# Recurrent block in two halves: projections and gates by turns, crossing gate tiles in pairs of 64 rows, low parts and products from GpSimd to VectorE

## The chip, the cores and the metric

The kernel runs on one core of a Trainium2 chip. The metric is device time in microseconds (us) of one execution; the kernel before took 1205.96 us (median of 3 runs, 1204.94 to 1206.43). Engines are named as in the profile: PE is TensorE (PEld its weight loads), DVE is VectorE, ACT is ScalarE, POOL is GpSimd, SP issues the DMAs.

## The reference, cut to what matters

The program is one inference step of a two-layer trunk: 256 prompt tokens and 32 sample tokens, 288 columns in all, share the weights. Each layer does a half-step FFN, a mixer, a second half-step FFN and a gated per-layer embedding, with an RMSNorm ahead of each. The mixer of layer 0 is attention, that of layer 1 the recurrent block that the change rewrites:

```python
def lru_mixer(xn, h0, conv0, w_in, conv_w, conv_b, w_a, b_a, w_x, b_x, lam, w_o):
    gx = xn @ w_in                                   # D_MODEL 1024 -> 2 * D_RNN (1280 each)
    gate = jax.nn.gelu(gx[..., :D_RNN])              # "g"
    u = gx[..., D_RNN:]                              # "u"
    ext = jnp.concatenate([conv0, u], axis=1)
    c = conv_b + sum(ext[:, j:j + T] * conv_w[j] for j in range(CONV_W))      # 4 taps
    cb = c.reshape(B, T, LRU_BLOCKS, LRU_BLOCK)      # 16 blocks of 80
    r = sigmoid(einsum('btnj,njk->btnk', cb, w_a) + b_a)                      # gate a
    gin = sigmoid(einsum('btnj,njk->btnk', cb, w_x) + b_x)                    # gate x
    log_a = (-LRU_C * softplus(-lam)) * r
    a = exp(log_a)
    bterm = sqrt(-expm1(2.0 * log_a)) * (gin * c)
    bterm = bterm.at[:, 0].add(a[:, 0] * h0)
    _, h = lax.associative_scan(_lin_combine, (a, bterm), axis=1)
    y = (h * gate) @ w_o
    return y, h[:, -1], new_conv
```

## The kernel before

**Tiling.** Features lie on the 128 partitions, tokens in the free dimension. D_MODEL is 8 chunks of 128 rows, D_RNN is 10, which the gates and the scan take in two halves of 5. Convolution and gates have 292 columns, since the sample's history lies between the two groups of tokens. Every float32 product is three matmuls (`product`, L1148): high part of the weights by high part of the data (L1154), high by low (L1155), low by high (L1156). The low part of a datum is the value less its rounded copy.

**Groups of weights.** The work of all stages is a row of groups, each with 10 to 16 weight tiles of 128x128 and a slot of its own of two (`raw0`/`raw1`, `w_hi0`/`w_hi1`, `w_lo0`/`w_lo1`). For each group SP loads `raw`, ACT copies it to `w_hi` (L513), DVE subtracts to `w_lo` (L784); both do it in two parts, one group ahead of PE and interleaved by hand with the stage's own instructions. ACT may write a slot when PE is through with the group that held it (`tiles_done`), and PE starts a group's first part when the first `w_lo` stands. The order of the work on each engine is written out by hand, in one `step` function for each engine; semaphores tie the engines together.

**The recurrent block** is stage 5. Its four phases run one after the other:
- `lru_in`, 5 groups: u for two chunks each (48 matmuls). DVE scales the two products into `u_ext` (L1044, L1046), ACT starts the convolution (L663), and DVE adds three taps (L908), those of one group in the period of the next. ACT rounds the finished chunk to `c_hi` (L757), POOL subtracts to `c_lo` (L462).
- `gates`, 4 groups (a and x of the first half, a and x of the second): each is 13 tiles, 39 matmuls of 128 rows. The blocks are 80 wide, so 8 of the 13 tiles lie across a border of chunks ("crossing") and have weights in one half of their rows alone; the other 5 are a chunk's own. ACT takes the sigmoids (L685) and loads its table (L655) ahead of them.
- `lru_g`, 5 groups: g, two chunks each. Beside it run tanh, exp and sqrt of the rates on ACT (L731 to L746), squares, addend and scans on DVE (L928, L937, L921), GELU on ACT (L751), the product y on POOL (L476, L477), its high part on ACT (L761) and its low part on DVE (L914).
- `lru_o`, 8 groups of 30 matmuls: the output. Groups 0 to 3 hold two output chunks and one half of k each, so that four chunks are done after group 3; groups 4 to 7 hold one whole chunk each. Behind a finished chunk DVE adds to `x_res` (L807), ACT and DVE make the next norm's input (L518, L793), and POOL adds the squares (L388, L385).

The next phase is the FFN `up3`. Its first group takes the first 7 chunks of x for both its outputs before the last one; behind it stands the matmul of the mean of squares (L1169).

Of the kernel before, what the change touches and what calls it, by code (L numbers as in the profile page):

```python
# [11 lines left out]
P = 128  # L12
# [6 lines left out]
SEQ = 256  # L19
# [32 lines left out]
U_GROUPS = [(("u", m), ("u", m + 1)) for m in range(0, KR, 2)]  # L52
G_GROUPS = [(("g", m), ("g", m + 1)) for m in range(0, KR, 2)]
U_OF = [[m for side, m in group] for group in U_GROUPS]
GELU_AT = [range(0, 6), range(6, 8), range(8, KR)]
# [24 lines left out]
def plan():  # L80
# [4 lines left out]
    def ple(n, stage):  # L85
# [6 lines left out]
    phases += [Phase("lru_in", 5, len(U_GROUPS), 2 * KD, body=len(U_GROUPS), counted=True),  # L92
               Phase("gates", 5, 4, BAND_TILES, body=4),
               Phase("lru_g", 5, len(G_GROUPS), 2 * KD, body=len(G_GROUPS), counted=True),
               Phase("lru_o", 5, KD, KR, body=KD)]
# [10 lines left out]
QKV, WO, LRU_G = (next(p for p in PHASES if p.name == name) for name in ("qkv", "wo", "lru_g"))  # L106
# [36 lines left out]
def in_array(tile):  # L143

    for name, groups in (("lru_in", IN_FIRST), ("lru_g", IN_LAST)):
        for n, group in enumerate(groups):
            if tile in group:
                return name, n, group.index(tile)

# [17 lines left out]
def build(nc, a):  # L167
    ctx = ExitStack()
    with ctx:
# [117 lines left out]
        gate_summed, gate_read = sem("gate_summed"), sem("gate_read")  # L287
        s_done, gated_used, tanh_done, a_done = sem("s_done"), sem("gated_used"), sem("tanh_done"), sem("a_done")
        a_square_done, b_square_done, b_root_done = sem("a_square_done"), sem("b_square_done"), sem("b_root_done")
        addend_done, start_set, gap_zeroed = sem("addend_done"), sem("start_set"), sem("gap_zeroed")  # L290
# [6 lines left out]
        def group_dram(phase, i):  # L297
# [4 lines left out]
            if kind == "ple":  # L302
                return a[kind][one(i + int(layer_ffn) * phase.groups)]
            return a[phase.name][one(i)]

# [18 lines left out]
        def _(sp):  # L324
# [8 lines left out]
            for phase in PHASES:  # L333
                def load(turn, n, b, phase=phase):
# [11 lines left out]
                    if phase.kind in ("lru_in", "lru_g"):  # L346
                        for o, landed in enumerate((lru_landed, raw_landed)):
                            name, g, at = in_array((U_GROUPS if phase.kind == "lru_in" else G_GROUPS)[n][o])
                            sp.dma_start(raw[slot_of(phase, b)][:, o * KD * P:(o + 1) * KD * P],
                                         a[name][g, :, at * KD * P:(at + 1) * KD * P]) \  # L350
                                .then_inc(landed[slot_of(phase, b)], 16)
                        return
                    if phase.name in SEAMS and turn is None and n == 0:
# [26 lines left out]
        def _(pool):  # L380
# [79 lines left out]
            with pool.Fori(0, KR) as m:  # L460
                pool.wait_ge(c_hi_done, m + 1)
# [4 lines left out]
            for half in range(2):  # L466
                pool.wait_ge(a_done, half + 1)
                nc.gpsimd.memset(rate[:, half * HALF:(half + 1) * HALF, SAMPLE - 1:SAMPLE], 0.0) \
                    .then_inc(gap_zeroed, 1)

            for m in range(KR):
                pool.wait_ge(gelu_done, next(n + 1 for n, ms in enumerate(GELU_AT) if m in ms))
                pool.wait_ge(h_done, m + 1)
                if m >= HALF:
                    pool.wait_ge(y_done, m - HALF + 1)
                nc.gpsimd.tensor_tensor(y_now[m % HALF][:, 0:SEQ], u_ext[:, m, 0:SEQ], gate_g[:, m, 0:SEQ], ALU.mult)  # L476
                nc.gpsimd.tensor_tensor(y_now[m % HALF][:, SEQ:TOK], u_ext[:, m, SAMPLE:SAMPLE + DEC],  # L477
                                        gate_g[:, m, SEQ:TOK], ALU.mult).then_inc(y_prod, 1)


# [11 lines left out]
        def _(act):  # L492
            def w_split(target, part):
# [9 lines left out]
                of_lru = phase.kind in ("lru_in", "lru_g")  # L503
                if of_lru and part == 0:
                    act.wait_ge(lru_landed[slot], ((n if phase.kind == "lru_in" else len(U_GROUPS) + n) // 2 + 1) * 16)
# [72 lines left out]
            for at_phase, phase in enumerate(PHASES):  # L578
# [3 lines left out]
                def step(turn, n, b, phase=phase, after=after, stage=stage, kind=kind):  # L582
# [70 lines left out]
                    elif kind == "lru_in":  # L653
                        if n == phase.groups - 1:
                            nc.scalar.preload_act_table_set("sigmoid_and_others")  # L655
                        part(nxt, 0)
                        part(nxt, 1)
                        if n == 0:
# [3 lines left out]
                        for m in U_OF[n]:  # L662
# [3 lines left out]
                        conv_high(n - 1)  # L666
                    elif kind == "gates":
                        half, is_x = n // 2, n % 2
                        ms = slice(half * HALF, (half + 1) * HALF)
                        if n == 3:  # L670
                            act.wait_ge(gated_used, 1)
                        for m in range(HALF):
                            q = n * HALF + m
                            if m < HALF - 1:
                                act.wait_ge(gate_summed, n * (HALF - 1) + m + 1)
                            else:
                                part(nxt, 0)
                                part(nxt, 1)
                                if n == 0:
# [870 lines left out]
```

## Time and profile before

| | us |
|---|---|
| median of 3 runs | 1205.96 |
| profiled execution | 1206.72 |
| its span, first to last instruction | 1204.6 |
| PE busy | 1178.3 (98%) |
| DVE / ACT / POOL busy | 795.4 / 584.4 / 170.3 |
| from the mean in the block's first u group to the mean behind `lru_o` | 833.05 to 954.28 |

The mean granted TensorE clock is 0.993 of full speed. Of the chain that ended last 90% is PE, 5% DVE and 3% ACT, so whatever isn't a matmul counts only where PE stands still. Matmul durations are latencies: the matmuls overlap, and what one costs is the distance from one start to the next.

### The profile page before, as it was taken

What the parts mean: (1) busy time and instruction counts of PE and PEld (TensorE: products, weight loads), DVE (VectorE), ACT (ScalarE), POOL (GpSimd) and SP (SyncE); (2) the same over time, 40 slices, a digit from 0 to 9 for tenths busy, and PEclk for the clock granted to TensorE, in tenths of its full rate; (3) what the DMA queues carried; (4) which work ended last, traced back from release to release, by engine and by line L of the source; (5) the groups of instructions that cost most, each with busy time, mean ns of one, the idle gap of its engine ahead of it and who ended that gap; (6) DMA issues with size and microseconds to landing.
All of it is one profiled execution on the core that took longest, in us unless ns stands there. A gap on an engine that the chain in (4) does not pass through costs nothing.

```text
span 1204.6 us, 23286 instructions
## 1 busy us (share of the span) xinstructions
PE 1178.3 (98%) x8952; PEld 1168.4 (97%) x8952; DVE 795.4 (66%) x1170; ACT 584.4 (49%) x862; POOL 170.3 (14%) x201
## 2 busy tenths in 40 slices
PE   6999999999999999999999999999999999999996
PEld 6999999999989999999999999999999999999995
DVE  7666555677758665565785566456989856655566
ACT  6444433466645444343564444335695544443353
POOL 3000002211123000011230000021306300000222
PEclk9999999999999999999999999999999999999998
DMA  6544444743335445444455444446453554544542
GB/s 211 198 147 168 153 147 166 257 138 121 106 114 200 154 170 174 140 146 165 157 196 175 153 161 152 150 163 187 134 189 113 195 180 156 174 153 143 170 152 87
DMA packets 37627, 193.19 MB, mean 160 GB/s; under 512 B 4001, under 2 KB 6321, under 8 KB 26049
## 3 DMA queue, kind: packets, MB, share of 16 engines
q1 hardware_dynamic: 36528, 187.86, 46.5%
q0 software_dynamic: 1040, 4.51, 1.1%
q8 instruction: 42, 0.69, 0.2%
q14 instruction: 17, 0.13, 0.0%
HBM read 188.78 MB, written 3.58 MB: 160 GB/s over the span
## 4 chain that ended last, share of the span: by engine, by line
PE 90%; DVE 5%; ACT 3%; issue 1%; DMA 1%; SPq 0%; DVEq 0%; ACTq 0%
PE bank L1154 30%; PE bank L1156 29%; PE bank L1155 29%; DVE w_lo L784 2%; ACT w_hi L513 1%; DVE conv L908 1%; DMA raw<-in_up 1%; PE bank L1185 0%; DVE u_ext L921 0%; PE bank L1169 0%; DVE stay L849 0%; DVE logit L841 0%; DVE conv L937 0%; ACT stay L555 0%; ACT stay L552 0%
## 5 line engine op out<-in xcount | busy, mean ns | idle before, releaser
L513 ACT ACTIVATE w_hi<-raw 128x1024 fp32r<-128x1024 f32 (+2 forms) x410 | 370.4, 927 | 341.0 <-PE bank L1156 327.0
L784 DVE TENSOR_TENSOR w_lo<-raw,w_hi 128x1024 fp32r<-128x1024 f32 (+2 forms) x410 | 457.5, 1134 | 85.5 <-ACT w_hi L513 82.6
L1154 PE MATMUL bank<-xg_hi,w_hi 128*128 128x288 f32 x1536 | 458.8, 299 | 9.3 <-DVE w_lo L815 8.3
L1155 PE MATMUL bank<-xg_lo,w_hi 128*128 128x288 f32 x1536 | 454.5, 296 | 0.0
L1156 PE MATMUL bank<-xg_hi,w_lo 128*128 128x288 f32 x1536 | 453.0, 295 | 0.0
L1154 PEld LDWEIGHTS bank<-xg_hi,w_hi 128*128 128x128 f32 x1536 | 289.0, 188 | 11.2 <-issue 8.0
L1156 PEld LDWEIGHTS bank<-xg_hi,w_lo 128*128 128x128 f32 x1536 | 290.5, 189 | 0.0
L1155 PEld LDWEIGHTS bank<-xg_lo,w_hi 128*128 128x128 f32 x1536 | 289.7, 189 | 0.4
L1154 PE MATMUL bank<-h_hi,w_hi 128*128 128x288 f32 x704 | 208.4, 296 | 0.0
L1155 PE MATMUL bank<-h_lo,w_hi 128*128 128x288 f32 x704 | 207.7, 295 | 0.0
L1156 PE MATMUL bank<-h_hi,w_lo 128*128 128x288 f32 x704 | 207.0, 294 | 0.0
L963 DVE TENSOR_TENSOR gate_in<-bank,rstd 128x288 f32<-128x288 f32 x88 | 40.2, 457 | 177.8 <-PE bank L1156 177.6
L1156 PEld LDWEIGHTS bank<-h_hi,w_lo 128*128 128x128 f32 x704 | 132.6, 188 | 0.0
L1155 PEld LDWEIGHTS bank<-h_lo,w_hi 128*128 128x128 f32 x704 | 132.2, 188 | 0.0
L1154 PEld LDWEIGHTS bank<-h_hi,w_hi 128*128 128x128 f32 x704 | 131.9, 187 | 0.0
L1154 PE MATMUL bank<-xg_side_hi,w_hi 128*128 128x288 f32 x352 | 104.6, 297 | 0.0
L1155 PE MATMUL bank<-xg_side_lo,w_hi 128*128 128x288 f32 x352 | 103.8, 295 | 0.0
L1156 PE MATMUL bank<-xg_side_hi,w_lo 128*128 128x288 f32 x352 | 103.5, 294 | 0.0
L395 POOL TENSOR_TENSOR sum_squares<-x_res 128x288 f32<-128x288 f32 x8 | 6.2, 778 | 610.1 <-DVE x_res L807 610.1
L518 ACT ACTIVATE xg_hi<-x_res,vecs_sb 128x288 fp32r<-128x288 f32 (+1 forms) x56 | 28.9, 533 | 129.0 <-DVE x_res L807 126.0
L388 POOL TENSOR_TENSOR square<-x_res 128x288 f32 (+1 forms) x58 | 44.7, 770 | 241.6 <-DVE x_res L807 240.1
L1156 PEld LDWEIGHTS bank<-xg_side_hi,w_lo 128*128 128x128 f32 x352 | 66.3, 188 | 0.0
(185 smaller groups left out, 1246.2 us busy)
## 6 DMA issues: line engine op xcount, KB each, us to landing
raw<-in_up SPq DMA_DIRECT2D x85, 1024.0 KB, 4.9
raw<-in_down SPq DMA_DIRECT2D x64, 704.0 KB, 4.0
raw<-in_qkv SPq DMA_DIRECT2D x24, 512.0 KB, 4.6
raw<-in_ple SPq DMA_DIRECT2D x16, 640.0 KB, 3.9
raw<-in_lru_in SPq DMA_DIRECT2D x12, 512.0 KB, 4.8
raw<-in_lru_o SPq DMA_DIRECT2D x8, 640.0 KB, 3.9
raw<-in_wo SPq DMA_DIRECT2D x4, 1024.0 KB, 5.3
raw<-in_lru_g SPq DMA_DIRECT2D x8, 512.0 KB, 4.4
```

The lines of the kernel that those rows point to most:

```text
L388: nc.gpsimd.tensor_tensor(square[:], x[:, k, :], x[:, k, :], ALU.mult).then_inc(squared, 1)
L395: nc.gpsimd.tensor_tensor(sum_squares[:], x[:, 0, :], x[:, 0, :], ALU.mult).then_inc(summed_squares, 1)
L513: nc.scalar.activation(w_hi[slot][:, cols], raw[slot][:, cols], ACT.Copy).then_inc(w_hi_done, 1)
L518: nc.scalar.activation(xg_of(stage)[0][:, k, :], x[:, k, :], ACT.Copy, scale=gain[:, stage, one(k)]) \
L784: nc.vector.tensor_tensor(w_lo[slot][:, cols], raw[slot][:, cols], w_hi[slot][:, cols].bitcast(F32), ALU.subtract).then_inc(w_lo_done, 1)
L908: nc.vector.scalar_tensor_tensor(out=conv[:, m, :], in0=u_ext[:, m, tap:tap + CW], scalar=vec["conv_w"][:, one(tap * KR + m)], in1=conv[:, ...
L963: nc.vector.tensor_tensor(gate_in[:], first, rstd[:], ALU.mult).then_inc(gate_in_done, 1)
L1154: nc.tensor.matmul(out, w_hi[slot][:, cols], hi[:, k, 0:width], start=start, stop=False)
L1155: nc.tensor.matmul(out, w_hi[slot][:, cols], lo[:, k, 0:width], start=False, stop=False)
L1156: return nc.tensor.matmul(out, w_lo[slot][:, cols], hi[:, k, 0:width], start=False, stop=stop)
```

## The change

1. **Order.** The phases become `lru_in` (u0, u1, u2, g0), `gates0` (a, x of the first half), `lru_mid` (u3, u4, g1), `gates1`, `lru_g` (g2, g3, g4), `lru_o`. A half's gates, rates and scan can start before the other half's u is there. All taps of a u group are now in that group's own period.
2. **Crossing tiles in pairs.** A gate group is now 5 own tiles (15 matmuls of 128 rows) and 8 crossing tiles as 24 matmuls of 64 rows, in 12 pairs on the lower and the upper rows of the array. Rows and pairs alternate as own 0 to 3, beside 0 and 1, own 4, beside 2 and 3.
3. **POOL to DVE.** `c_low` and `y_full` (the subtraction and the product that POOL did) are DVE instructions; POOL's memset of the rates' gap goes. A scan is now two (256 and 32 columns) with `h0` as start of the second, so the copy of `h0` goes.
4. **`lru_o` by halves.** Groups 0 to 3 hold two output chunks each with the first half of k, groups 4 to 7 the same chunks with the second half. All of x's chunks are then done in groups 4 to 7, two behind each.
5. **Smaller ones.** One multiplication by a broadcast operand for five rates; GELU in two parts, not three; ACT loads 7 tables in stage 5, not 4; the weights of the block's projections land in two pieces; the first group of `up3` takes 6 chunks first, then the last 2.

```diff
-U_GROUPS = [(("u", m), ("u", m + 1)) for m in range(0, KR, 2)]
-G_GROUPS = [(("g", m), ("g", m + 1)) for m in range(0, KR, 2)]
+LRU_GROUPS = {"lru_in": (("u", 0), ("u", 1), ("u", 2), ("g", 0)), "lru_mid": (("u", 3), ("u", 4), ("g", 1)),
+              "lru_g": (("g", 2), ("g", 3), ("g", 4))}
+GATE_BANKS = (4, 5, 6, 7, 0, 1, 4, 5, 2, 3, 4, 5, 6, 7, 2, 3, 0, 1, 4, 5)
+GATE_ORDER, LAST_STEP = (0, 2, 4, 1, 3), (0, 3, 2, 3, 2)
...
+                def own(m):
+                    gate_bank_free(group, m)
+                    if tile_of[m, m] >= phase.part_a:
+                        pe.wait_ge(w_lo_done, 2 * (phase.first_group + n) + 2)
+                    pe.wait_ge(c_done, first + m + 1)
+                    product(out[m], slot, tile_of[m, m], (c_hi, c_lo), first + m, CW, True, False)
+                def beside(step, below, above):
+                    if step > 1:
+                        pe.wait_ge(beside_done, 3 * group + step - 1)
+                    for w, c in ((w_hi, c_hi), (w_hi, c_lo), (w_lo, c_hi)):
+                        for rows, (m, k) in zip(HALF_ROWS, (below, above)):
+                            cols = slice(tile_of[m, k] * P, (tile_of[m, k] + 1) * P)
+                            last = nc.tensor.matmul(out[m], w[slot][rows, cols], c[rows, first + k, :], start=False,
+                                                    stop=w is w_lo and step == LAST_STEP[m])
+                    return last.then_inc(tiles_done if step == 3 else beside_done, 1)
+                pe.wait_ge(w_lo_done, 2 * (phase.first_group + n) + 1)
+                for m in range(HALF - 1):
+                    own(m)
+                beside(0, (0, 1), (2, 1))
+                beside(1, (1, 2), (3, 2))
+                own(HALF - 1)
+                beside(2, (2, 3), (4, 3))
+                beside(3, (3, 4), (1, 0))
...
-                nc.gpsimd.tensor_tensor(c_lo[:, m, :], conv[:, m, :], c_hi[:, m, :].bitcast(F32), ALU.subtract) \
-                    .then_inc(c_done, 1)
+            def c_low(group):
+                for m in U_OF[group]:
+                    dve.wait_ge(c_hi_done, m + 1)
+                    nc.vector.tensor_tensor(c_lo[:, m, :], conv[:, m, :], c_hi[:, m, :].bitcast(F32), ALU.subtract) \
+                        .then_inc(c_done, 1)
...
 def o_chunks(n):
-    return () if n < 2 else (2 * n - 4, 2 * n - 3) if n < KD // 2 else (n,)
+    return () if n < KD // 2 else (2 * n - KD, 2 * n - KD + 1)
```

On PE, the start of a gate group before: each output bank takes its two or three tiles one after the other, all of 128 rows (lines 1154 to 1156 are `product`).

```order
L1154 MATMUL bank4<-c_hi,w_hi1 128x292
L1155 MATMUL bank4<-c_lo,w_hi1 128x292
L1156 MATMUL bank4<-c_hi,w_lo1 128x292
L1154 MATMUL bank4<-c_hi,w_hi1 128x292
L1155 MATMUL bank4<-c_lo,w_hi1 128x292
L1156 MATMUL bank4<-c_hi,w_lo1 128x292
L1154 MATMUL bank5<-c_hi,w_hi1 128x292
```

On PE, the first gate group now, from the last of its first four own tiles (lines 1231 to 1233 are `product`, 1340 is the 64-row matmul of `beside`).

```order
L1233 MATMUL bank7<-c_hi,w_lo0 128x292
L1340 MATMUL bank4<-c_hi,w_hi0 128x292
L1340 MATMUL bank6<-c_hi,w_hi0 128x292
L1340 MATMUL bank4<-c_lo,w_hi0 128x292
L1340 MATMUL bank6<-c_lo,w_hi0 128x292
L1340 MATMUL bank4<-c_hi,w_lo0 128x292
L1340 MATMUL bank6<-c_hi,w_lo0 128x292
L1340 MATMUL bank5<-c_hi,w_hi0 128x292
L1340 MATMUL bank7<-c_hi,w_hi0 128x292
```

The two matmuls of a pair write different banks, and both lie between 128-row matmuls of the same group.

On ACT, from the last u group ahead of the first gates but one to the first sigmoids, before: `c_hi` is the rounding, L655 the table, `w_hi` of 896 and 768 the weights of a gate group.

```order
L757 ACTIVATE c_hi<-conv 128x292 x2
L513 ACTIVATE w_hi<-raw 128x896
L513 ACTIVATE w_hi<-raw 128x768
L663 ACTIVATE conv<-u_ext,vecs_sb 128x292 x2
L757 ACTIVATE c_hi<-conv 128x292 x2
L655 ACT_TABLE_LOAD
L513 ACTIVATE w_hi<-raw 128x896
L513 ACTIVATE w_hi<-raw 128x768
L663 ACTIVATE conv<-u_ext,vecs_sb 128x292 x2
L757 ACTIVATE c_hi<-conv 128x292 x2
L685 ACTIVATE rate<-bank,vecs_sb 128x292 x4
```

The same place now, from the last u group ahead of the first gates: `c_hi` is the rounding, L684 the table, `w_hi` the weights of the group x and then of u3 (128x1024).

```order
L676 ACTIVATE conv<-u_ext,vecs_sb 128x292 x2
L528 ACTIVATE w_hi<-raw 128x768
L789 ACTIVATE c_hi<-conv 128x292 x2
L684 ACT_TABLE_LOAD
L528 ACTIVATE w_hi<-raw 128x896
L528 ACTIVATE w_hi<-raw 128x768
L756 ACTIVATE rate<-bank,vecs_sb 128x292 x3
L528 ACTIVATE w_hi<-raw 128x1024
L756 ACTIVATE rate<-bank,vecs_sb 128x292 x2
L528 ACTIVATE w_hi<-raw 128x1024
L756 ACTIVATE gated<-bank,vecs_sb 128x292 x5
```

The table stands between the rounding of a u group and the weights of gate group x in both. Before, that u group was the fourth, whose taps ran in the period of the fifth, ahead of the gates; now it is the third, the last ahead of the gates, with g0 between.

On DVE, the end of `lru_o` before: `x_res` is the addition to x, `xg_lo` the low part of the next norm's input, `w_lo` of 640 the weights of `lru_o`, of 1024 those of `up3`.

```order
L807 SCALAR_TENSOR_TENSOR x_res<-bank,x_res 128x288
L784 TENSOR_TENSOR w_lo<-raw,w_hi 128x640
L793 SCALAR_TENSOR_TENSOR xg_lo<-x_res,vecs_sb,xg_hi 128x288
L784 TENSOR_TENSOR w_lo<-raw,w_hi 128x640
L807 SCALAR_TENSOR_TENSOR x_res<-bank,x_res 128x288
L784 TENSOR_TENSOR w_lo<-raw,w_hi 128x1024
L793 SCALAR_TENSOR_TENSOR xg_lo<-x_res,vecs_sb,xg_hi 128x288
L784 TENSOR_TENSOR w_lo<-raw,w_hi 128x1024
L807 SCALAR_TENSOR_TENSOR x_res<-bank,x_res 128x288
L793 SCALAR_TENSOR_TENSOR xg_lo<-x_res,vecs_sb,xg_hi 128x288
L784 TENSOR_TENSOR w_lo<-raw,w_hi 128x1024 x2
```

The same place now:

```order
L839 SCALAR_TENSOR_TENSOR x_res<-bank,x_res 128x288 x2
L816 TENSOR_TENSOR w_lo<-raw,w_hi 128x640 x2
L825 SCALAR_TENSOR_TENSOR xg_lo<-x_res,vecs_sb,xg_hi 128x288 x2
L839 SCALAR_TENSOR_TENSOR x_res<-bank,x_res 128x288 x2
L825 SCALAR_TENSOR_TENSOR xg_lo<-x_res,vecs_sb,xg_hi 128x288 x2
L816 TENSOR_TENSOR w_lo<-raw,w_hi 128x1024 x2
L839 SCALAR_TENSOR_TENSOR x_res<-bank,x_res 128x288 x2
L825 SCALAR_TENSOR_TENSOR xg_lo<-x_res,vecs_sb,xg_hi 128x288 x2
L816 TENSOR_TENSOR w_lo<-raw,w_hi 128x1024 x2
```

Each of the last four groups now has two chunks of x where it had one, and in the last two groups the weights come behind both.

## Rows read from the trace of the kernel before

**Rows 1.** Page, busy time of the engines, with share and instruction count.

```profile
PE 1178.3 (98%) x8952; PEld 1168.4 (97%) x8952; DVE 795.4 (66%) x1170; ACT 584.4 (49%) x862; POOL 170.3 (14%) x201
```

**Rows 2.** Timeline, PE: start, duration, engine, line, out<-in, count; the two means.

```profile
832.65 0.29 PE L1154 MATMUL bank<-xg_hi,w_hi 128*128 128x288 f32 x1
...
833.05 0.65 PE L1169 MATMUL bank<-sum_squares,mean_w 128*128 128x288 f32 x2
...
833.67 0.29 PE L1155 MATMUL bank<-xg_lo,w_hi 128*128 128x288 f32 x1
...
954.28 0.65 PE L1169 MATMUL bank<-sum_squares,mean_w 128*128 128x288 f32 x2
```

**Rows 3.** Timeline, PE: a gate group running through, 30 matmuls apart.

```profile
859.13 0.30 PE L1154 MATMUL bank<-c_hi,w_hi 128*128 128x292 f32 x1
...
863.15 0.29 PE L1154 MATMUL bank<-c_hi,w_hi 128*128 128x292 f32 x1
```

**Rows 4.** Timeline, PE: wait and restart inside the gates.

```profile
869.44 0.29 PE L1156 MATMUL bank<-c_hi,w_lo 128*128 128x292 f32 x1
870.24 0.40 PE L1154 MATMUL bank<-c_hi,w_hi 128*128 128x292 f32 x1 [0.50 <-DVE w_lo L784]
870.48 0.30 PE L1155 MATMUL bank<-c_lo,w_hi 128*128 128x292 f32 x1
```

**Rows 5.** Timeline, PE: first group of lru_o.

```profile
913.79 0.29 PE L1156 MATMUL bank<-y_hi,w_lo 128*128 128x288 f32 x1
914.98 0.40 PE L1154 MATMUL bank<-y_hi,w_hi 128*128 128x288 f32 x1 [0.89 <-DVE y_lo L914]
...
916.45 0.40 PE L1154 MATMUL bank<-y_hi,w_hi 128*128 128x288 f32 x1 [0.81 <-DVE y_lo L914]
```

**Rows 6.** Timeline, PE: three 128-row transposes; then the 64-row pairs of the scores.

```profile
257.25 0.55 PE L1213 MATMUL bank<-ident,v_all 128*128 128x128 f32 x3 [1.22 <-DVE v_rows L868]
257.55 0.38 PE L1154 MATMUL bank<-xg_hi,w_hi 128*128 128x288 f32 x1
...
266.55 0.25 PE L1202 MATMUL bank<-stay_lo,ones 128*128 128x192 f32 x1
266.73 1.53 PE L1185 MATMUL bank<-q_all,k_all 64*128 64x128 f32 x24
...
268.42 0.29 PE L1155 MATMUL bank<-xg_lo,w_hi 128*128 128x288 f32 x1
```

**Rows 7.** Timeline, DVE: one u group.

```profile
846.53 0.42 DVE L1044 TENSOR_TENSOR u_ext<-bank,rstd 128x256 f32<-128x256 f32 x1 [0.58 <-PE bank L1156]
...
847.40 1.19 DVE L908 SCALAR_TENSOR_TENSOR conv<-u_ext,vecs_sb,conv 128x292 f32<-128x292 f32 x2
848.51 1.21 DVE L784 TENSOR_TENSOR w_lo<-raw,w_hi 128x1024 fp32r<-128x1024 f32 x1
849.65 0.94 DVE L908 SCALAR_TENSOR_TENSOR conv<-u_ext,vecs_sb,conv 128x292 f32<-128x292 f32 x2
```

**Rows 8.** Timeline, ACT: rounding, table and weights ahead of the gates.

```profile
858.39 0.88 ACT L757 ACTIVATE c_hi<-conv 128x292 fp32r<-128x292 f32 x2 [2.67 <-DVE conv L908]
859.29 1.28 ACT L655 ACT_TABLE_LOAD   x1
860.59 1.69 ACT L513 ACTIVATE w_hi<-raw 128x896 fp32r<-128x896 f32 x2
```

**Rows 9.** Timeline, DVE: a low part of one chunk.

```profile
924.78 0.44 DVE L914 TENSOR_TENSOR y_lo<-up_in,y_hi 128x288 fp32r<-128x288 f32 x1
```

**Rows 10.** Timeline, DVE: two-chunk groups of lru_o, then the weights of up3.

```profile
928.05 0.82 DVE L807 SCALAR_TENSOR_TENSOR x_res<-bank,x_res 128x288 f32<-128x288 f32 x2 [1.20 <-PE bank L1156]
...
929.93 1.90 DVE L793 SCALAR_TENSOR_TENSOR xg_lo<-x_res,vecs_sb,xg_hi 128x288 fp32r<-128x288 f32 x2
...
936.99 0.45 DVE L807 SCALAR_TENSOR_TENSOR x_res<-bank,x_res 128x288 f32<-128x288 f32 x1
...
945.71 1.86 DVE L784 TENSOR_TENSOR w_lo<-raw,w_hi 128x1024 fp32r<-128x1024 f32 x1 [1.04 <-ACT w_hi L513]
```

More of the change, by code:

```diff
@@ L148, in in_array, with in_two_pieces, first_pieces @@
                 return name, n, group.index(tile)
+def in_two_pieces(phase, n):
+    return phase.name in LRU_GROUPS or phase.name == "lru_o" and isinstance(n, int) and n % (KD // 2) >= KD // 4
+def first_pieces(phase, n):
+    group = phase.first_group + n
+    return sum(in_two_pieces(p, i) and p.first_group + i <= group and (p.first_group + i) % 2 == group % 2
+               for p in PHASES for i in range(p.groups if p.stage == 5 else 0))
 def index(turn, n, per_turn):
@@ new lines, in y_full, with gelu_inputs @@
+            def y_full(m):
+                dve.wait_ge(gelu_done, next(n + 1 for n, ms in enumerate(GELU_AT) if m in ms))
+                dve.wait_ge(h_done, m + 1)
+                if m >= HALF:
+                    dve.wait_ge(y_done, m - HALF + 1)
+                nc.vector.tensor_tensor(y_now[m % HALF][:], u_ext[:, m, 0:TOK], gate_g[:, m, :], ALU.mult) \
+                    .then_inc(y_prod, 1)
+            def gelu_inputs(group, products):
+                for m, product in zip(G_OF[group], products):
+                    last = nc.vector.tensor_tensor(gate_g[:, m, :], product, rstd[:], ALU.mult)
+                last.then_inc(pair_free, 1)
@@ L1237, in mix, with gates @@
                 last.then_inc(mixed, 1)
+            def gates(phase, n, slot):
+                group = 2 * int(phase.name[-1]) + n
+                first = group // 2 * HALF
+                out = [bank[GATE_BANKS[group * HALF + m]][:, 0:CW] for m in range(HALF)]
+                tile_of = {pair: at for at, pair in enumerate((m, k) for m in range(HALF) for k in BAND[m])}
+                low, high = HALF_ROWS
+                def own(m):
[21 more added lines that the diff above has]
+                beside(3, (3, 4), (1, 0))
@@ new lines, in gate_bank_free @@
+            def gate_bank_free(group, m):
+                at = GATE_BANKS[group * HALF + m]
+                earlier = [g * HALF + GATE_ORDER.index(j) + 1 for g in range(group) for j in range(HALF)
+                           if GATE_BANKS[g * HALF + j] == at]
+                if earlier:
+                    pe.wait_ge(gate_read, earlier[-1])
+                if at < 4:
+                    pe.wait_ge(pair_free, LRU_IN.first_pair + (3 if at < 2 else 4) if group < 2 else
+                               LRU_MID.first_pair + (3 if at < 2 else 2))
```

423 lines of the change are left out of this document (225 added, 198 removed).

## The prediction, made before the changed kernel ran

> **What bounds the kernel now.** I read the page first: PE is busy 1178.3 of 1204.6 us [rows 1], so only two things can move the time: fewer or cheaper matmuls, and the stretches in which PE stands still. Then I read PE's timeline through the recurrent block. The reader is to see the two matmuls of the mean, one in the block's first u group and one behind `lru_o`, at 833.05 and 954.28 us [rows 2]: 121.23 us apart. Between them lie 15 groups' worth of projections, 720 matmuls of 288 columns, and 156 gate matmuls of 292. A 288-column matmul costs 0.1333 (three in 0.40 us ahead of the first mean) [rows 2], a 292-column one 0.134 (30 in 4.02) [rows 3]. That is 96.0 + 20.9, and the mean adds 0.49 (0.62 to the second matmul behind it, less one pitch) [rows 2]: 117.4. So PE now **loses 3.8 us** in the block. The largest pieces are a wait in the gates (0.80 from start to start where 0.134 is due) [rows 4] and the waits for the low part of y in the first group of `lru_o` (1.19, and 1.47 over three matmuls, where 0.13 and 0.40 are due) [rows 5]. After a wait the first matmul costs 0.24 and not 0.134, so its weight load shows as 0.1 more [rows 4]. Last I read DVE and ACT in the same stretches, for the chains on which PE will wait.
>
> **The change part by part.**
>
> *Pairs.* 24 crossing matmuls of 128 rows a gate group, 96 in all, become 48 pairs. The trace has such pairs in the scores: 24 matmuls of 64 rows and 128 columns in 1.53 us, which is 0.128 a pair with the last one's latency in it, and about 0.11 without [rows 6]. A 128-row matmul of 128 columns costs 0.10 there (three in 0.30) [rows 6]. So a pair costs 1.1 to 1.3 of one matmul, not two. For 292 columns that bounds a pair at 0.134 (the pitch of one) below and 0.174 (1.3 of it) above; I take 0.14, near the low end, since the longer figure holds a latency. Gain: 48 x (0.268 - 0.14) = **-6.1**, bounds -4.5 and -6.4.
>
> *Switches.* Rows and pairs alternate, four switches a group, 16 in all. From the last 128-row matmul ahead of the scores to the second behind them it is 1.87 us (266.55 to 268.42) [rows 6]. In it lie a 192-column matmul (0.09 in proportion), 12 pairs at 0.11 and one pitch: 1.54. So two switches cost 0.33; with pairs at 0.10 it is 0.45, with 0.128 only 0.11. I take 0.19 each, **+3.0**, bounds 1.0 and 3.6. A cheap pair goes with a dear switch, since both come out of the same 1.87. The rule that speaks against the change is in the Trainium skill, page "TensorEngine Tiling (Array Packing)", section "Key Properties": a change of tiling mode drains the engine. The trace agrees, with those 0.33 us for two.
>
> *The waits that go.* POOL's subtraction and product are gone from the chains of [rows 4] and [rows 5]; I take all **3.8** off and put in what the new order makes late.
>
> *The gates of the first half.* Per u group DVE now has four scalings (0.87, 846.53 to 847.40), two `w_lo` of 1024 (1.14 each, 848.51 to 849.65), six taps (0.43 each) [rows 7] and two low parts of c (0.37, priced as a low part of 0.44 less the overlap of neighbours) [rows 9]: 6.5 us, against 48 x 0.1333 = 6.4 on PE. It doesn't catch up. u0 is scaled from about 836.3; with its taps in its own period it is through at 842.0, where before it took u1 at 840.1; u1 ends at 848.5; u2's last taps (four scalings, two low parts, two `w_lo` of a gate group at 1.0 and 0.87, six taps: 6.1) at 854.6. Behind them ACT rounds, loads its table and splits the weights of gate group x: 0.9 until the table (858.39 to 859.29), 1.3 for it, 0.95 for the first part [rows 8], where the table starts behind the second rounding. That is 857.4, and DVE's first `w_lo` ends near 858.5. PE enters the gates one u group earlier than at 859.13 [rows 3], at 852.7, and group a takes 15 x 0.134 + 12 x 0.14 + 4 x 0.19 = 4.4: it is at x from 857.1, 1.4 too early. Four own tiles on, the third output of x wants the bank of a's fourth sigmoid; that stands behind a `w_hi` of 1024 on ACT: another 1.0. Together **+2.4**, bounds 0.8 (the table covered by an ACT that is early) and 3.2. Queued behind that `w_hi` are all later sigmoids and with them DVE's rates, which nobody needs at once. The second half has its taps two groups earlier; I give its wait for the last c 0.4.
>
> *`lru_o`'s front.* Five scans, five products and low parts (0.37 each [rows 9]) stand on DVE ahead of groups 0 and 1, interleaved with weights; POOL no longer stretches them. Before, the two longest waits alone cost 1.05 each [rows 5]. I take +1.6 for the front and the start of group 4 together, bounds 0 and 3.
>
> *The seam to `up3`.* All eight chunks now end in the last four groups, two behind each. Before, a two-chunk group took DVE 4.47 ((936.99 - 928.05) / 2) [rows 10], since POOL's squares stretch its work (0.95 for an `xg_lo` [rows 10] where a low part takes 0.44 [rows 9]); PE needs 30 x 0.1333 = 4.0. From the end of group 4 as zero, DVE is at group 6 at 0.35 + 2 x 4.47 = 9.3, through with two additions and two `xg_lo` at 11.9, and with the first `w_lo` of `up3` (1.2, or 1.86 beside POOL [rows 10]) at 13.1 to 13.8. PE stands before `up3` at 12.0. With signal and restart 1.4 to 2.1, and 0.3 for a later mean: **+2.0**, bounds 0 and 4.1 (every DVE instruction of the last two groups as slow as the 1.86). The 6-and-2 order of chunks covers the last two `xg_lo`, not this `w_lo`.
>
> *At no cost.* The broadcast multiplication, the longer GELU and the three more table loads (1.3 each [rows 8]) lie beside g groups, where ACT has half its time free; without that cover a load costs 1.3. The split scans and the pieces of the loads move no instruction onto PE's path.
>
> *Sum.* -6.1 + 3.0 - 3.8 + 2.4 + 0.4 + 1.6 + 2.0 = **-0.5 us**. Against the profiled execution, 1206.72, that is 1206.2; against the median of the runs, 0.76 lower, **1205.5**.
>
> **The rivals.**
>
> *A. The chains run ahead.* The new waits come to 3.4 and not 6.4: POOL is idle until `lru_o`, so DVE runs at its bare pitches, ACT reaches the table early, and the seam's squares cost less than in [rows 10]. For it: each wait of the block before [rows 4, 5] hung on an operation that POOL made or stretched. Against: DVE's 6.5 on 6.4 leaves no room for catching up. -3.5, so 1202.5.
>
> *B. A pair shows its weight loads.* If the next pair's loads can't run under the matmuls of the pair before, a pair costs what a first matmul costs, 0.24 [rows 4], in place of 0.14: 48 x 0.1 = 4.8 more. A longer group a covers 1.2 of the wait at x, so the sum is -0.5 + 4.8 - 1.2 = +3.1, and 1209.1. It decides from a pair of 0.21 on, where the sum passes 2.4. Against it: pairs at 0.11 to 0.13 [rows 6], below 0.24 with their shorter stream. The Trainium skill, page "TensorE: Matmul & The Clock Gate", section "The mechanism" of Part 3, says that weight loads overlap running matmuls only where the row groups differ, which would be B for the same half of successive pairs. The trace contradicts it for 128 rows, where the pitch of 0.134 leaves no room for a load shown as 0.1.
>
> *C. The seam takes its upper bound,* 4.1 in place of 2.0: +1.6, so 1207.6. For it: POOL has two squares and two sums a group right beside the `w_lo`. Against: in [rows 10] only one of the instructions shown there doubles.
>
> **How the numbers follow.** The measurement can tell about 0.2% from no change, 2.4 us: under 1203.55 is faster, over 1208.4 slower. Forecast 0.50, A 0.26, B 0.09, C 0.15. Faster takes most of A and a little of the forecast, whose own range is 1203.2 to 1207.8: 0.27. Slower takes B, a third of C and a little of the forecast: 0.18. The rest, 0.55, is the same. The range is 1202.4 to 1208.8: from A down to its value, and past C to the near side of B.
>
> **What would show it.** Pairs: two `beside` matmuls start within some ns of each other and the next pair 0.14 later. Switches: about 0.2 more at each of the 16 changes. Gates: PE idle ahead of the x group of the first half for a `w_lo`, then for a sigmoid of the a group. Seam: the first matmul of `up3` waiting 1.4 to 2.1 for a `w_lo`. `lru_o`'s first group without waits over 1 us. From mean to mean it should be about 120.7. The prediction is wrong if a pair costs over 0.2, if that seam waits for 4 us, or if PE goes through the gates without the two waits.

## The result: 0.27% slower, just outside the range

The changed kernel takes 1208.95 us (median of 9 runs, 1206.25 to 1211.41), the kernel before 1205.91 in the runs beside it: ratio 1.0027, 95% interval 1.0015 to 1.0038. It was forecast at 1205.5 with a range to 1208.8, and "slower" at 0.18. A second set gave 1207.92 (12 runs) against 1206.38, ratio 1.0017 [1.0008, 1.0026], which lies inside the range. The profiled execution took 1208.36, with a span of 1206.6.

The profile after, PE's timeline (start, duration, line, count, wait before it): the two means and, between them, the first gate groups.

```profile
832.96 0.65 PE L1246 MATMUL bank<-sum_squares,mean_w 128*128 128x288 f32 x2
...
855.73 0.30 PE L1233 MATMUL bank<-c_hi,w_lo 128*128 128x292 f32 x1
855.96 0.41 PE L1340 MATMUL bank<-c_hi,w_hi 64*128 64x292 f32 x2
856.20 0.30 PE L1340 MATMUL bank<-c_lo,w_hi 64*128 64x292 f32 x2
...
856.73 0.30 PE L1340 MATMUL bank<-c_hi,w_lo 64*128 64x292 f32 x2
858.47 0.41 PE L1231 MATMUL bank<-c_hi,w_hi 128*128 128x292 f32 x1 [1.44 <-DVE w_lo L816]
...
859.25 0.29 PE L1233 MATMUL bank<-c_hi,w_lo 128*128 128x292 f32 x1
860.59 0.46 PE L1231 MATMUL bank<-c_hi,w_hi 128*128 128x292 f32 x1 [1.05 <-ACT rate L756]
860.85 0.45 PE L1232 MATMUL bank<-c_lo,w_hi 128*128 128x292 f32 x1
861.09 0.45 PE L1233 MATMUL bank<-c_hi,w_lo 128*128 128x292 f32 x1
...
863.58 0.45 PE L1340 MATMUL bank<-c_hi,w_lo 64*128 64x292 f32 x2
...
956.59 0.69 PE L1246 MATMUL bank<-sum_squares,mean_w 128*128 128x288 f32 x2
```

From mean to mean it is 123.63 us, where [rows 2] had 121.23 and the forecast 120.7: the loss is in the block. The reader is to see four things. A pair costs 0.133 (856.20 to 856.73 is four), the pitch of one whole matmul in [rows 3]. A switch costs 0.20: 0.23 and 0.24 at 855.73 and 855.96, where 0.134 each is due. The two waits forecast in the gates are there, for the operations that were named, 1.74 and 1.34 from start to start. And behind the second one the matmuls start 0.24 to 0.26 apart and last 0.45, not 0.30, until 863.58. That isn't a wait. It is the clock, as the windows of the same trace say (stretch, length, PE busy, granted clock, DMA share, GB/s):

```profile
858.00:860.00 2.00, 1.07 (x6) 1.00 0.06 18
860.00:862.00 2.00, 1.41 (x6) 0.70 0.46 100
862.00:864.00 2.00, 2.00 (x15) 0.50 0.92 281
864.00:866.00 2.00, 2.00 (x19) 0.95 0.84 227
```

For 3.4 us (1.2 + 2.0 + 0.2 by these rows) PE has half the granted clock, the lower of its two levels (1.2 GHz and not 2.4). The other waits of the block: for c in the second half, for y and the weights in `lru_o`, and at the seam.

```profile
886.04 0.29 PE L1233 MATMUL bank<-c_hi,w_lo 128*128 128x292 f32 x1
886.87 0.38 PE L1231 MATMUL bank<-c_hi,w_hi 128*128 128x292 f32 x1 [0.54 <-DVE c_lo L953]
...
914.39 0.29 PE L1233 MATMUL bank<-y_hi,w_lo 128*128 128x288 f32 x1
915.05 0.40 PE L1231 MATMUL bank<-y_hi,w_hi 128*128 128x288 f32 x1 [0.36 <-DVE y_lo L946]
...
918.73 0.30 PE L1233 MATMUL bank<-y_hi,w_lo 128*128 128x288 f32 x1
919.44 0.40 PE L1231 MATMUL bank<-y_hi,w_hi 128*128 128x288 f32 x1 [0.41 <-DVE w_lo L816]
...
931.33 0.30 PE L1233 MATMUL bank<-y_hi,w_lo 128*128 128x288 f32 x1
932.06 0.41 PE L1231 MATMUL bank<-y_hi,w_hi 128*128 128x288 f32 x1 [0.43 <-DVE w_lo L816]
...
948.03 0.29 PE L1233 MATMUL bank<-y_hi,w_lo 128*128 128x288 f32 x1
950.13 0.37 PE L1231 MATMUL bank<-xg_hi,w_hi 128*128 128x288 f32 x1 [1.80 <-DVE w_lo L816]
```

Why PE waits in the gates is in ACT's timeline (after), which answers to [rows 8]: rounding, table, the weights of group x, three sigmoids, a `w_hi` of u3, and only then the sigmoid that frees the bank.

```profile
854.14 0.88 ACT L789 ACTIVATE c_hi<-conv 128x292 fp32r<-128x292 f32 x2 [2.57 <-DVE conv L940]
855.05 1.28 ACT L684 ACT_TABLE_LOAD   x1
856.34 1.68 ACT L528 ACTIVATE w_hi<-raw 128x896 fp32r<-128x896 f32 x2
857.93 1.27 ACT L756 ACTIVATE rate<-bank,vecs_sb 128x292 f32<-128x292 f32 x3
859.09 1.06 ACT L528 ACTIVATE w_hi<-raw 128x1024 fp32r<-128x1024 f32 x1
860.03 0.90 ACT L756 ACTIVATE rate<-bank,vecs_sb 128x292 f32<-128x292 f32 x2
```

### The profile page after: what moved, and what is told of

The parts are those of the page before. It is cut to its first block, busy times and chain, and to the rows that moved or that the text cites. A ratio compares the mean times of both kernels' runs of the same rounds, so it can differ in the third digit from the quotient of the medians.

```text
span 1206.6 us, 23246 instructions
## 1 busy us (share of the span) xinstructions
PE 1176.6 (98%) x8952; PEld 1163.6 (96%) x8952; DVE 797.1 (66%) x1192; ACT 588.0 (49%) x864; POOL 144.0 (12%) x169
## 4 chain that ended last, share of the span: by engine, by line
PE 86%; DVE 8%; ACT 4%; issue 1%; DMA 0%; SPq 0%; DVEq 0%; ACTq 0%
PE bank L1231 28%; PE bank L1233 28%; PE bank L1232 28%; DVE w_lo L816 3%; ACT w_hi L528 1%; DVE conv L940 1%; DVE xg_lo L825 1%; PE bank L1340 0%; PE bank L1262 0%; DVE u_ext L981 0%; DMA x_res<-in_x 0%; PE bank L1246 0%; DVE stay L881 0%; DVE logit L873 0%; ACT stay L570 0%
## 5 line engine op out<-in xcount | busy, mean ns | idle before, releaser
L528 ACT ACTIVATE w_hi<-raw 128x1024 fp32r<-128x1024 f32 (+3 forms) x410 | 370.7, 926 | 333.4 <-PE bank L1233 328.9
L816 DVE TENSOR_TENSOR w_lo<-raw,w_hi 128x1024 fp32r<-128x1024 f32 (+3 forms) x410 | 458.1, 1135 | 87.7 <-ACT w_hi L528 84.9
```

What stands on the lines that cost most here:

```text
L528: nc.scalar.activation(w_hi[slot][:, cols], raw[slot][:, cols], ACT.Copy).then_inc(w_hi_done, 1)
L816: nc.vector.tensor_tensor(w_lo[slot][:, cols], raw[slot][:, cols], w_hi[slot][:, cols].bitcast(F32), ALU.subtract).then_inc(w_lo_done, 1)
```

## The experiments

The theory: the waits are worth about what was forecast, and what isn't in the forecast is the clock, which falls behind a long wait of PE. The rival: the waits alone, larger than they were sized, make the loss, and the clock is a by-product that costs nothing. Ratios are to the kernel before in runs on the same chip, with 95% intervals.

**Extra matmuls in the waits of the gates.** They need no data that is late, so they end no wait; they keep PE busy in it.

```diff
+                if group == 1:
+                    gate_bank_free(group, 0)
+                    for _ in range(3):
+                        nc.tensor.matmul(out[0][:, 0:TOK], mean_w[:], sum_squares[:], start=True, stop=True)
                 pe.wait_ge(w_lo_done, 2 * (phase.first_group + n) + 1)
...
+                    if group == 1 and m == 2:
+                        gate_bank_free(group, 4)
+                        for _ in range(2):
+                            nc.tensor.matmul(out[4][:, 0:TOK], mean_w[:], sum_squares[:], start=True, stop=True)
                     own(m)
```

> The changed kernel, with five extra matmuls of the mean (288 columns, two passes of 0.24 us each, results overwritten) put in front of the two waits of gate group x of the first half: three (1.45 us) ahead of the wait for w_lo, two (0.97 us) ahead of the wait for the sigmoid. They take no data that is late, so the waits end when they did. Clock theory: in the trace of the changed kernel 860.6 to 864 us ran at half the granted clock right behind the two waits (1.5 and 1.3 us); with PE busy in them the clock stays, PE goes through these groups 1.4 us earlier, from mean to mean 122.2 us in place of 123.6, ratio to the kernel before about 1.0013 in place of 1.0027. Rival, waits alone: what is lost is the waits, the clock falls for another reason or costs nothing; half clock is still seen, or the distance from mean to mean stays at 123.6.

Ratio 1.0013 [1.0004, 1.0022], as the clock theory had it. But from mean to mean it was 123.68, as the rival had it, so this run alone decides nothing. The clock stays at 1.00 through the gates and falls elsewhere, behind the wait at the seam (same views, this kernel):

```profile
945.99 0.29 PE L1233 MATMUL bank<-y_hi,w_lo 128*128 128x288 f32 x1
948.08 0.37 PE L1231 MATMUL bank<-xg_hi,w_hi 128*128 128x288 f32 x1 [1.80 <-DVE w_lo L816]
948.29 0.29 PE L1232 MATMUL bank<-xg_lo,w_hi 128*128 128x288 f32 x1
...
948.97 0.44 PE L1233 MATMUL bank<-xg_hi,w_lo 128*128 128x288 f32 x1
```

```profile
948.00:950.00 2.00, 1.92 (x10) 0.65 0.00 0
950.00:952.00 2.00, 2.00 (x10) 0.50 0.65 139
```

The same wait of 2.1 us had left the clock alone in the trace above. So a long wait can be followed by half clock, and need not be.

**ACT reordered ahead of the gates** (weights of group x ahead of the rounding of u2 and the table; the sigmoid of chunk 1 ahead of the next `w_hi`).

```diff
-                        conv_high(group)
+                        if group != 2:
+                            conv_high(group)
                     elif kind in ("lru_in", "lru_mid"):
-                        nc.scalar.preload_act_table_set("sigmoid_and_others")
+                        if kind == "lru_mid":
+                            nc.scalar.preload_act_table_set("sigmoid_and_others")
                         part(nxt, 0)
                         part(nxt, 1)
+                        if kind == "lru_in":
+                            conv_high(2)
+                            nc.scalar.preload_act_table_set("sigmoid_and_others")
...
-                        for m in GATE_ORDER[:3]:
+                        for m in GATE_ORDER[:4]:
...
-                        for m in GATE_ORDER[3:]:
+                        for m in GATE_ORDER[4:]:
```

> The changed kernel with two places on ACT reordered: the weights of gate group x of the first half are split ahead of the rounding of u2 and the table load, and in both halves the sigmoid of chunk 1 of group a stands ahead of the next w_hi. Clock theory with waits: the wait for w_lo (1.5) goes to about 0.4 ahead of chunk 4, the wait for the sigmoid (1.3) to about 0.4, and the half clock (1.4) goes with them: mean to mean 120.2, ratio to before about 0.999. Waits alone: 121.6, ratio 1.0005, and half clock seen somewhere. Rival, DVE is the bound of the first half: the waits come back one place on, at the next group's w_lo; mean to mean stays above 122.5.

1204.37 us, ratio 0.9988 [0.9978, 0.9998], mean to mean 120.34. Both waits are short now (0.51 and 0.35 from start to start, this kernel), and no stretch of the block has less than the full clock:

```profile
853.50 0.30 PE L1345 MATMUL bank<-c_hi,w_lo 64*128 64x292 f32 x2
854.01 0.37 PE L1236 MATMUL bank<-c_hi,w_hi 128*128 128x292 f32 x1 [0.22 <-DVE c_lo L958]
...
856.35 0.30 PE L1238 MATMUL bank<-c_hi,w_lo 128*128 128x292 f32 x1
856.70 0.40 PE L1236 MATMUL bank<-c_hi,w_hi 128*128 128x292 f32 x1
```

So the change is worth having, by 0.1%, once ACT's order goes with it; the third rival, DVE as the bound of the first half, would have kept mean to mean above 122.5.

**Crossing tiles whole, not in pairs.**

```diff
-                        for rows, (m, k) in zip(HALF_ROWS, (below, above)):
+                        for m, k in (below, above):
                             cols = slice(tile_of[m, k] * P, (tile_of[m, k] + 1) * P)
-                            last = nc.tensor.matmul(out[m], w[slot][rows, cols], c[rows, first + k, :], start=False,
+                            last = nc.tensor.matmul(out[m], w[slot][:, cols], c[:, first + k, :], start=False,
```

> The changed kernel with the crossing gate tiles as single 128-row matmuls in the same order and with the same waits (same results, no pairs, no change of tiling). If pairs are worth 48 x 0.134 = 6.4 and the 16 switches cost 3.1, PE has 3.3 us more to do, 0.8 a gate group; group a of the first half then covers 0.8 of the 1.5 us wait at x, and with a wait of 0.7 and not 1.5 ahead of the next one the clock stays (1.4): net +1.0, mean to mean 124.6. If the clock falls all the same: +2.4, 126.0. Rival, switches eat the pairs: mean to mean below 123.6.

Ratio 1.0025 [1.0015, 1.0035], mean to mean 124.30 with the full clock all through. In time the pairs bring nothing that can be measured beside the 1.0027 and 1.0017 of the changed kernel. Of the 3.2 us that pairs save on PE after their switches, the trace keeps 2.1 (124.3 against an estimated 122.2, the changed kernel's 123.63 less 1.45 for its fall), since the longer groups cover waits: the one ahead of group x is 0.70 here and not 1.74.

**Weights of `up3` ahead of the low parts.**

```diff
+                        if n == KD - 2:
+                            part(nxt, 0)
                         for m in o_chunks(n):
                             xg_low(stage + 1, m)
-                        if n >= KD - 2:
+                        if n == KD - 2:
+                            part(nxt, 1)
+                        if n == KD - 1:
                             part(nxt, 0)
                             part(nxt, 1)
```

(On ACT likewise, both parts ahead of the rounding.)

> The changed kernel with the first weights of up3 split ahead of the rounding and low parts of x behind group 6 of lru_o (first part ahead, second behind on DVE; both ahead on ACT). If DVE's order makes the wait of 2.0 us at up3, it falls to about 1.0, spread over w_lo and the low parts of the last chunks: mean to mean 122.6, ratio to before 1.0018. Rival, the pair of DVE and POOL is the bound there whatever the order: the wait moves to the low parts of the last chunks and stays near 2.0; mean to mean 123.6.

Ratio 1.0008 [0.9998, 1.0017], more of a gain than expected. The wait at `up3` is gone, and 1.1 of it comes back at the mean, which waits for POOL's sums of squares. Mean to mean is 121.44, without a fall in the block; against the estimated 122.2 that is 0.8 for the edit, where 1.0 was expected. Its trace has the two waits in the gates, and behind them **no** fall:

```profile
858.88 0.40 PE L1238 MATMUL bank<-c_hi,w_hi 128*128 128x292 f32 x1 [1.44 <-DVE w_lo L819]
...
861.01 0.40 PE L1238 MATMUL bank<-c_hi,w_hi 128*128 128x292 f32 x1 [1.05 <-ACT rate L759]
861.25 0.30 PE L1239 MATMUL bank<-c_lo,w_hi 128*128 128x292 f32 x1
...
862.79 0.29 PE L1347 MATMUL bank<-c_hi,w_lo 64*128 64x292 f32 x2
```

From the start behind the second wait to the last pair ahead of the next switch it is 1.78 us here and 2.99 in the changed kernel's own trace: 1.2 for the fall up to there, 1.45 with the switch and restart behind it.

**The changed kernel again.**

> The changed kernel once more, unchanged. In the trace of the run with the weights of up3 ahead of the low parts the clock stayed up with the same two waits in the gates (1.73 and 1.35 us from start to start). Theory: the fall of the clock behind these waits doesn't come in every execution; this trace may show it or not, the waits are the same to 0.05 us either way, and the distance from mean to mean is 123.6 with it and 122.2 without. Timed: ratio 1.0025 +- 0.0010. Rival: the clock falls whenever this kernel runs, and was kept up in that run by its edit; then it is seen here again.

The waits are the same (1.74 and 1.35), the clock falls behind them again, mean to mean 123.59. With the trace before, it fell in two of the three that had these waits.

**Both reorderings.**

> The changed kernel with both reorderings, that of ACT ahead of the gates and that of the first weights of up3. If the two gains are in different places and add up (0.9988 and 1.0008 against 1.0027): ratio to before 0.997, mean to mean 119.6 (120.3 less 0.8). Rival: what is gained in the gates is given back at the seam or the other way round; 0.9985 or above.

1204.05 us, 0.9981 [0.9972, 0.999], mean to mean 120.40, 0.8 more than expected. In the trace nothing is left of the second gain (120.34 with ACT's reordering alone), and the two ratios, 0.9981 and 0.9988, overlap, so that the gains add up isn't shown. The 1.1 us wait at the mean stays, and the wait for c in the second half grew from 0.83 to 1.24: with PE early, the chain of u3 and u4 is late.

**Five edits together** (also the x groups' own tiles in one run, the addend behind weights, the mean four tiles later).

```diff
-                for m in range(HALF - 1):
+                for m in range(HALF - 1 + n):
                     own(m)
                 beside(0, (0, 1), (2, 1))
                 beside(1, (1, 2), (3, 2))
-                own(HALF - 1)
+                if n == 0:
+                    own(HALF - 1)
...
-                        mean(stage)
+                        if phase.name != "up3":
+                            mean(stage)
...
-                            addend(1)
                             part(nxt, 0)
                             part(nxt, 1)
+                            addend(1)
...
+                            if phase.name == "up3" and n == 1 and turn is None and tile == 4:
+                                mean(stage)
```

> Both reorderings, and three more: in the two x gate groups all five own tiles stand ahead of one run of pairs, so that 4 of the 16 switches go (0.19 each by the trace of the changed kernel: 0.8); the addend of the second half stands behind the weights of lru_o's group 1 (its wait, 0.58); the mean of stage 6 stands four tiles into up3's second group (the wait for POOL's squares, 1.0). All together 2.3 less than with the two reorderings alone: mean to mean (the second mean comes 1.6 later by its place) 119.6 + 1.6 - 2.3 = 118.9, ratio 0.995. Rival: the own tile of chunk 4 then waits for its bank or its weights and takes back the 0.8, and the scans move the wait to a later group of lru_o: 0.9965.

0.9978 [0.9968, 0.9989], a miss: mean to mean 122.15. Moving the addend took the wait of group 1 away and raised that of group 4 from 0.73 to 1.54. The wait for c was 1.93 in this trace, partly because the first `w_hi` of the u groups behind the gates waited 0.7 for its DMA, and behind it the clock fell:

```profile
884.56 0.38 PE L1243 MATMUL bank<-c_hi,w_hi 128*128 128x292 f32 x1 [1.64 <-DVE c_lo L961]
```

```profile
884.00:888.00 4.00, 3.44 (x22) 0.72 0.70 240
```

**ACT reordered, crossing tiles whole** (the edits of the second and third experiments).

> The reordering of ACT ahead of the gates, and the crossing tiles as single 128-row matmuls (no pairs, no switches, same results). With the waits of the gates gone nothing covers the longer groups: 48 x 0.134 - 16 x 0.19 = 3.4 more on PE than the reordering alone, less the 0.5 wait for chunk 4 at most: mean to mean 120.3 + 3.0 = 123.3, ratio 1.0013. Rival: pairs bring less than their count because switches also delay what follows; below 1.0003.

Ratio 1.0015 [1.0006, 1.0023], where the pairs had 0.9988 [0.9978, 0.9998]. Here the pairs show in time, 0.27% or some 3.3 us. The trace has 123.86, with a fall behind the seam's wait (0.50 at 950 to 952); without that, 1.5, it is about 122.4, 2.0 more than with pairs. The rest of the 3.3 isn't shown to be the pairs: the granted clock of the timed runs is 0.9935 here and 0.9951 with pairs in the mean, which is about one fall a run more (the next experiment says how a fall shows in this figure).

**Extra matmuls in all three long waits** (those of the first experiment, and eight at the seam).

```diff
+                    if phase.name == "up3" and turn is None and n == 0:
+                        for _ in range(8):
+                            nc.tensor.matmul(pair[0][:, 0:P], mean_w[:], mean_w[:], start=True, stop=True)
                     if phase is not PHASES[0] or turn is not None or n > 0:
                         pe.wait_ge(w_lo_done, parts + 1)
```

> The changed kernel with extra matmuls in all three long waits: those of the run with the filled gates, and eight of mean_w by itself (128 columns, 1.7 us) ahead of the wait for w_lo at up3. In the trace with the gates alone filled the clock fell behind the wait at up3 (948 to 952 us at half, 1.5 us lost) and not behind the gates. Clock theory: no half clock anywhere in the block, waits as before, mean to mean 122.2; ratio to before 1.0005 to 1.001, below the 1.0013 of the gates alone. Rival: the clock falls at another place of the block as often; 1.0013 or above.

0.9996 [0.9987, 1.0005], below both intervals of the changed kernel. The waits end when they did (1.73 and 1.35 from start to start in the gates; 1.89 at the seam, 0.2 less), PE has more to do, no stretch of the block has half the clock, and mean to mean is 122.1. The seam of this kernel, with the matmuls in it:

```profile
945.94 1.95 PE L1469 MATMUL bank<-mean_w 128*128 128x128 f32 x16
947.70 0.40 PE L1231 MATMUL bank<-xg_hi,w_hi 128*128 128x288 f32 x1
947.94 0.29 PE L1232 MATMUL bank<-xg_lo,w_hi 128*128 128x288 f32 x1
```

This settles that the clock is part of the loss: the rival allows no gain from work that ends no wait. The timed runs say the same. For each the mean granted clock was taken, and a fall of 3.4 us takes 0.0014 off it (half of 3.4 in 1205 us). In the mean it is 0.9928 and 0.9930 in the two sets of the changed kernel, 0.9943 to 0.9944 in the four sets of the kernel before, and 0.9961 here. So the changed kernel has about one fall a run more than the kernel before, and two more than with its waits filled. Time goes with it: of the timed runs of the kernel before, the 28 at 0.996 took 1205.0 us in the mean and the 36 at 0.993 or less 1207.1.

**Without the addend's move** (the five edits less that one).

> Both reorderings, all five own tiles ahead of one run of pairs in the two x gate groups, and the mean of stage 6 four tiles into up3's second group; the addend stays where the change has it. Against the kernel with five edits this gives the wait of lru_o's group 1 back (0.58) and takes that of group 4 back to 0.6 (it was 1.4). Against the two reorderings: 0.8 for four switches and 1.0 for the mean. Mean to mean 119.6 + 1.6 - 1.8 = 119.4 if the clock stays, ratio 0.9965; if one long wait is left (that for c in the second half, 1.2 to 1.9) and the clock falls behind it in part of the runs, 0.997 to 0.998.

1203.09 us, 0.9977 [0.9968, 0.9987], mean to mean 120.58, not 119.4: the wait for c is 1.12 and the first group of `lru_o` waits 1.10 for y. With PE early, DVE's chain is the bound of the first group of `lru_o`: in this trace DVE runs without a pause from 900 to 911 us, scans, weights, products and low parts of y, while PE waits from 909.7 to 910.8.

**The kernel before, with its own long wait filled.** Looking for such falls elsewhere, I found one in the trace of before, in the attention:

```profile
335.79 0.25 PE L1202 MATMUL bank<-stay_lo,ones 128*128 128x192 f32 x1
337.98 0.55 PE L1213 MATMUL bank<-ident,v_all 128*128 128x128 f32 x3 [1.94 <-DVE v_rows L868]
...
339.19 0.44 PE L1156 MATMUL bank<-o_hi,w_lo 128*128 128x288 f32 x1
```

```profile
330.00:340.00 10.00, 8.06 (x83) 0.94 0.49 167
340.00:350.00 10.00, 10.00 (x83) 0.89 0.48 175
```

```diff
                 sum_stay(a)
+                pe.wait_ge(qkv_first_read, QKV.groups)
+                for _ in range(9):
+                    nc.tensor.matmul(bank[0][:, 0:P], mean_w[:], mean_w[:], start=True, stop=True)
                 turn_v(b)
-                pe.wait_ge(qkv_first_read, QKV.groups)
```

(The wait for `qkv_first_read` moves ahead of the extra matmuls.)

> The kernel before, with nine extra matmuls of mean_w by itself (128 columns, about 1.95 us together, overwritten later) in the wait of PE for v_rows at 335.8 us, in the attention. In the trace of the kernel before that wait is 2.19 us from start to start, and behind it 338.8 to 342 us run at half the granted clock; in the trace of the changed kernel with ACT reordered the same wait of 2.19 us is followed by the full clock, and the stretch from mean to mean around it is 144.2 us and not 145.7. Clock theory: with PE busy in the wait the stretch is 144.2 in every trace, and the time falls by up to 1.5 us: ratio 0.9988 to 0.9995. Rival: the clock there depends on something else; half clock is still seen, ratio 1.000.

0.9995 [0.9986, 1.0004]: at the edge of what was expected, and no gain that is clear by itself. The trace shows what it should, full clock behind the wait:

```profile
330.00:340.00 10.00, 10.00 (x105) 1.00 0.55 181
340.00:350.00 10.00, 10.00 (x103) 1.00 0.41 162
```

**The same in the kernel without the addend's move.**

> The kernel with both reorderings, the x gate groups' pairs in one run and the later mean (0.9977 before), with the same nine matmuls in the attention's wait. If the two gains add up: ratio 0.997 to 0.9975, mean to mean in the attention 144.2, in the block 120.6. Rival: that kernel had no fall of the clock in the attention anyway; 0.9977.

1201.45 us against 1206.63, ratio 0.9956 [0.9943, 0.997] (5 runs): more than expected, and the fastest here, ahead of both kernels. Mean to mean is 120.69; in the attention it is 144.22, where the kernel without the filling had 144.98 in a trace without a fall. The timed runs point to the clock for the rest: theirs is 0.9966 in the mean, four of the five at 0.997, as in its own trace, which has no fall, against 0.9948 in the eleven runs without the filling, about 1.3 falls a run. Which falls went with it isn't seen.

## Why the prediction was wrong

| term of the sum | forecast | measured |
|---|---|---|
| pairs | -6.1 | -6.4 (0.133 to 0.134 a pair) |
| switches | +3.0 | +3.2 (0.20 each) |
| waits that go | -3.8 | -3.8 |
| gates, first half | +2.4 | +2.8 (1.74 less a switch's 0.22; 1.34 less 0.13, with a restart) |
| c, second half | +0.4 | +0.8 |
| `lru_o`, front and group 4 | +1.6 | +2.5 |
| seam | +2.0 | +2.0 |
| granted clock | not in it | +1.45 |
| sum | -0.5 | +2.5 (mean to mean +2.4) |

**The step that failed** is the one on the gates of the first half: it priced the two waits at their length. In the changed kernel's traces they were followed by 3.4 us at half clock, 1.45 us more, half of the gap to the forecast (2.9 from mean to mean). Filled, these waits and the one at the seam cost about what the forecast had for them. That the filled kernel then is at 0.9996, by its ratio right on the forecast of 1205.5, is partly luck: its mean to mean of 122.1 is still 1.4 above the forecast's 120.7, and its timed runs had fewer falls than those of the kernel before (0.9961 against 0.9944). The clock was no rival either, though the trace of before had it from 338.8 us on. The page's row of the granted clock hides it (a slice of 30 us with 3.4 at half clock still shows a 9), and I opened no windows behind PE's longest waits.

**The second step, mis-sized,** is the front of `lru_o` with c: 3.3 and not 2.0. For it I took a figure between two bounds, 1.6 between 0 and 3, and did not follow which of DVE's instructions stand ahead of the first low part of y and of the weights of groups 1 and 4. The table loads "at no cost" belong here: they lie on ACT ahead of u3's rounding, and with PE early that chain is the late one (c waits 1.12 to 1.93 in the kernels with both reorderings, 0.82 with ACT's alone). That they make it late is argued from the order, since no run takes a load away.

**Right:** the pairs overlap fully, so rival B fails: a pair is 0.133, not 0.24. The Trainium skill's rule on switches (page "TensorEngine Tiling (Array Packing)", section "Key Properties") stands with 0.20 us each. Both waits in the gates came at the forecast operations, and the seam's within 0.1. One sum is printed wrong: 854.6 + 0.9 + 1.3 + 0.95 is 857.75, not 857.4; the 857.4 holds if only the second rounding, 0.45, lies behind the last tap, and so it came out (the table started at 855.05, the `w_lo` at 857.32). The lower bound of the switches, 0.11 for two, makes 0.9 and not 1.0. Neither changes the forecast. Rival A fails, since the waits came to 8.1, not 3.4; rival C in its size, 2.0 and not 4.1.

**Still open:** the medians moved by 3.0 and 1.5 us in two sets, the trace by 2.4 in the block. The granted clocks of the timed runs give about one fall a run more than before, but not where it lies; only the profiled executions show that. Why a wait of one length is followed by half clock in one execution and not in the next is open too.

## What to carry to other kernels

Price a wait of PE at its length plus what the clock may cost behind it (1.45 to 1.55 us here), and look in the trace of before, behind its longest waits, for what that was. Where a wait can't be taken away, cheap matmuls into a free bank kept the clock up in each of the four traces that had them. And an edit that gives PE less to do is worth no more than the slack of the chains that feed it: reorder those first, then the saving shows (0.9988 against 1.0015, part of it the clock).

## What the runs showed of the hardware

Waits of PE in the block and two of the attention, and the granted clock behind them in the profiled executions (us from start to start, without the waits that were filled):

| wait | clock fell in | stayed in |
|---|---|---|
| 1.7 and 1.35, 2.5 apart (gates) | 2 traces | 1 |
| 2.1 (seam) | 2 | 4 |
| 1.9 (c) | 1 | 0 |
| 2.2 (attention) | 10 | 2 |
| 1.5 to 1.7, single (an earlier one of the attention in 14 traces; group 4 of `lru_o` in one) | 0 | 15 |
| 0.7 and 1.35 (gates, whole tiles) | 0 | 1 |
| 1.24 or less (block) | 0 | all |

The length of one wait isn't the whole of it: at the start of the program half clock came back in three traces behind several shorter waits (before: 0.85, 0.60, 0.47 and 0.84 from start to start within 4 us, then 0.64 of the clock from 14 to 16 us). Each fall was to half the granted clock; the three that could be compared with a trace without one cost 1.45 to 1.55 us. Pairs of 64 rows and 292 columns cost no more than one matmul of 128 rows, where the scores' pairs of 128 columns had left 0.13 to 0.17 open.
